# The up-projections of a gated feed-forward block by Strassen's seven products of quarters, with the weights' sums made by GpSimd

## The chip, the cores and the metric

One core of one Trainium2 chip runs the whole kernel. The metric is the device time of one execution in microseconds (us), as the median of several.

## The reference

Two transformer blocks run over 512 tokens of width 1024 in float32. The change concerns two gated feed-forward layers of the second block, here called GLU 1 and GLU 2:

```python
D_FF_2 = 2816
def swiglu(x, w1, w3, w2):
    return (jax.nn.silu(x @ w1) * (x @ w3)) @ w2
...
h = h + 0.5 * swiglu(rms_norm(h, ffn1_norm[l]), ffn1_w1[l], ffn1_w3[l], ffn1_w2[l])   # GLU 1
...
h = h + 0.5 * swiglu(rms_norm(h, ffn2_norm[l]), ffn2_w1[l], ffn2_w3[l], ffn2_w2[l])   # GLU 2
```

w1 and w3 are 1024 x 2816 ("gate" and "up", both up-projections), w2 is 2816 x 1024.

## The kernel before, in words

Everything is kept transposed: features on the 128 partitions, the 512 tokens along the free dimension, in two halves of 256 tokens (`hf` 0 and 1, `F` for both). Every float32 operand is split into a high part in the fp32r type and a low rest: for weights ScalarE writes the high part (`act_hi`, a Copy) and VectorE the low one (`dve_lo`, raw minus high). One product is then three matmuls into the same PSUM region, high by high, high by low and low by high (`mm3`), each with its own weight load of 128 x 128.

Weights come by DMA from SP's queue, in the order of `PLAN`, into three raw slots of 8 KB a partition (`NRAW`). A slot is loaded again when VectorE has made the low part of what lay in it. The split weights lie in three pairs of buffers (`NW`); the high part of weight w waits for the last matmul that used weight w-3 (`("used", w - NW)`). `act_step` and `dve_step` call for the splits two weights ahead. All five engines run their instructions strictly in the order written in `act_program`, `dve_program` and so on; a wait holds back all that stands behind it on that engine.

In a GLU, `pe_gate` works in 11 chunks of 256 features. A chunk takes one weight tile of w1 and one of w3 (each 1024 x 256, so 2 tiles of 128 features by 8 slices of the 1024 inputs by 3 matmuls, 48 matmuls of 512 tokens). Chunk 0 is made in two halves of 256 tokens (96 matmuls of 256 columns for each half), because the RMS norm of the second half is still being worked out beside it (`act_opening`, `dve_opening`, `dve_normed`, `act_normed`, `pool_normed`, with two scratch tiles `td` that go round for the normed input). ScalarE applies SiLU out of PSUM, VectorE multiplies by the other projection, then the product is split in high and low again (`act_hidden`, `dve_hidden`). w2 follows in three blocks of 8, 8 and 6 slices (`pe_linear`), each block one stage of chunks later than the chunks that it uses, and the last four outputs of the last block again in halves of 256 tokens, so that the next norm can start. In GLU 1 VectorE also scales the residual stream X by the last norm of the first block, eight instructions that stand in `dve_glu` after the first four chunks. PSUM has eight banks, handed out in turn by `banks`. GpSimd does little in the GLUs: some of the low parts of the normed input (`pool_normed`).

## Time and profile before

| what | us |
| --- | --- |
| median of 3 runs | 2319.98 (2315.99 to 2324.92) |
| the profiled execution, its own time | 2314.78 |
| its span, from the first to the last instruction | 2313.0 |
| TensorE (PE) busy in the span | 2228.9 |
| VectorE (DVE) busy | 1173.9 |
| ScalarE (ACT) busy | 825.9 |
| GpSimd (POOL) busy | 179.8 |

Busy time of PE is modelled, since matmuls are pipelined: what one matmul costs is read from the distance between two events that matmuls release, not from its duration. PEld is the weight load. SP issues the DMAs. The granted clock is TensorE's clock as a share of 2.4 GHz: 1.00 is 2.4 GHz and 0.50 is 1.2 GHz. A few per cent of the matmul records are missing from the trace, so counts in windows are a little low. A row of the timeline merges neighbouring instructions of one line, and names the shape of the first alone.

### The profile page before, as it was taken

Reading aid. Unit: us, or ns where it says so; the run is one execution under the profiler, and the core shown is the slowest. Engines: PE = TensorE matmul, PEld = TensorE weight load, DVE = VectorE, ACT = ScalarE, POOL = GpSimd, SP = SyncE. Lnnn points to the kernel's source line nnn. Section 1 sums busy time; section 2 is a strip of 40 time slices with the busy share of each in tenths; the row PEclk is TensorE's granted clock in tenths of the full one; section 3 lists DMA queues with packets and bytes.
Section 4 is the critical chain, followed back from the end, with each engine's and each line's share of the span. In section 5 each row is a group of like instructions: output and inputs, shape, how many; then the busy total and the mean of one; then the engine's idle time right before and its main releaser. Section 6 shows DMA issues by size and latency. Waiting matters only on the chain.

```text
span 2313.0 us, 27926 instructions
## 1 busy us (share of the span) xinstructions
PE 2228.9 (96%) x11611; PEld 1886.9 (82%) x11611; DVE 1173.9 (51%) x1845; ACT 825.9 (36%) x1241; POOL 179.8 (8%) x155
## 2 busy tenths in 40 slices
PE   6998999999999899999999999999999999999998
PEld 3877988888897788888898888887778889888887
DVE  5676566556577664334353433344664445333334
ACT  3555342213256543223243222234443324222222
POOL 7210000000033000000020000002012001000000
PEclk8999999999999999999999999999999999999999
DMA  6442255555520222322313232224112331422320
GB/s 230 141 140 85 93 171 180 190 180 185 189 74 19 86 80 91 109 91 91 110 55 110 91 109 91 82 73 120 57 32 73 119 110 56 127 92 92 109 73 37
DMA packets 144099, 245.45 MB, mean 106 GB/s; under 512 B 4763, under 2 KB 69622, under 8 KB 143846
## 3 DMA queue, kind: packets, MB, share of 16 engines
q1 hardware_dynamic: 139216, 228.02, 29.7%
q0 software_dynamic: 4096, 15.28, 2.0%
q8 instruction: 92, 1.51, 0.3%
q10 hardware_dynamic: 662, 0.37, 0.1%
q14 instruction: 33, 0.27, 0.0%
HBM read 241.56 MB, written 2.10 MB: 105 GB/s over the span
## 4 chain that ended last, share of the span: by engine, by line
PE 88%; DVE 6%; ACT 3%; issue 1%; DMA 1%; POOL 0%; SPq 0%; DVEq 0%; ACTq 0%
PE PS L66 87%; ACT t L72 3%; DVE t L83 2%; DVE t L86 1%; DVE t L75 1%; PE PS L69 1%; DMA t<-in_w_ada_dram 1%; DVE t L79 1%; POOL t L75 0%; DVE t L92 0%; DVE t L80 0%; SPq L101 0%; DVE t L95 0%; ACT L72 0%; DVEq L58 0%
## 5 line engine op out<-in xcount | busy, mean ns | idle before, releaser
L66 PE MATMUL PS<-t,t 128*128 128x512 f32 (+4 forms) x11244 | 2180.0, 357 | 53.3 <-ACT t L72 16.3
L66 PEld LDWEIGHTS PS<-t,t 128*128 128x128 f32 (+2 forms) x11244 | 1844.1, 188 | 386.2 <-issue 61.3
L72 ACT ACTIVATE t<-t 128x2048 fp32r<-128x2048 f32 (+10 forms) x551 | 527.7, 972 | 1174.0 <-PE PS L66 691.3
L75 DVE TENSOR_TENSOR t<-t,t 128x2048 fp32r<-128x2048 f32 (+8 forms) x476 | 581.9, 1227 | 650.9 <-ACT t L72 648.8
L72 ACT ACTIVATE t<-PS 128x512 f32<-128x512 f32 (+5 forms) x307 | 162.3, 545 | 183.0 <-PE PS L66 123.5
L75 POOL TENSOR_TENSOR t<-t,t 128x512 f32<-128x512 f32 (+2 forms) x71 | 88.1, 1242 | 1136.7 <-ACT t L72 962.7
L83 DVE SCALAR_TENSOR_TENSOR t<-t,t,t 128x1024 f32<-128x1024 f32 (+2 forms) x149 | 140.5, 947 | 16.4 <-DMA t<-in_w_ada_dram 10.9
L72 ACT ACTIVATE t<-t,t 128x256 fp32r<-128x256 f32 (+5 forms) x212 | 112.4, 537 | 88.9 <-DVE t L83 45.7
L75 DVE TENSOR_TENSOR t<-t,PS 128x512 f32<-128x512 f32 (+2 forms) x92 | 54.6, 600 | 147.2 <-PE PS L66 140.8
L83 DVE SCALAR_TENSOR_TENSOR t<-PS,t,t 128x512 f32<-128x512 f32 (+3 forms) x120 | 76.9, 643 | 94.6 <-PE PS L66 84.7
L69 PE MATMUL PS<-t,t 128*128 128x128 f32 (+1 forms) x367 | 57.8, 296 | 26.9 <-DMA t<-in_x_dram 6.1
L69 PEld LDWEIGHTS PS<-t,t 128*128 128x128 f32 (+1 forms) x367 | 44.8, 151 | 35.6 <-issue 10.6
L83 DVE SCALAR_TENSOR_TENSOR t<-t,t,PS 128x256 f32<-128x256 f32 (+1 forms) x133 | 62.0, 488 | 21.0 <-PE PS L66 13.9
L83 DVE SCALAR_TENSOR_TENSOR t<-PS,t 128x512 f32<-128x512 f32 (+1 forms) x68 | 40.3, 595 | 59.2 <-PE PS L66 58.7
L75 DVE TENSOR_TENSOR t<-t 128x512 f32<-128x512 f32 (+3 forms) x99 | 56.6, 572 | 23.0 <-ACT t L72 22.4
L79 DVE TENSOR_SCALAR t<-t,t 128x128 f32<-128x128 f32 (+5 forms) x159 | 56.5, 388 | 5.2 <-DMA t<-in_w_ada_dram 2.7
L79 POOL TENSOR_SCALAR t<-t 128x512 f32<-128x512 f32 x28 | 46.5, 1659 | 72.8 <-DVE t L86 48.5
L86 DVE CUSTOM_DVE_ANT_0 t<-PS,t 128x128 f32<-128x128 f32 (+1 forms) x112 | 38.5, 352 | 16.0 <-PE PS L66 15.8
L75 DVE TENSOR_TENSOR t<-PS,t 128x512 fp32r<-128x512 f32 (+2 forms) x40 | 25.0, 634 | 33.9 <-ACT t L72 23.5
L101 POOL DMA_DIRECT2D t<-in_k_dist_dram x1 | 0.5, 543 | 427.3 <-PE PS L66 427.3
L86 DVE CUSTOM_DVE_ANT_0 t<-PS,t,t 128x384 f32<-128x384 f32 (+3 forms) x56 | 29.3, 522 | 2.0
L72 ACT ACTIVATE t<-PS,t 128x2 f32<-128x2 f32 (+3 forms) x44 | 19.0, 431 | 29.0 <-PE PS L66 28.4
(30 smaller groups left out, 154.2 us busy)
## 6 DMA issues: line engine op xcount, KB each, us to landing
t<-in_w_ff_dram SPq DMA_DIRECT2D x64, 1024.0 KB, 5.3
t<-in_ffn_w_dram SPq DMA_DIRECT2D x60, 1024.0 KB, 5.2
t<-in_w_ada_dram SPq DMA_DIRECT2D x36, 1024.0 KB, 6.1
t<-in_w_in_dram SPq DMA_DIRECT2D x13, 1024.0 KB, 5.0
t<-in_w_ada_dram POOLq DMA_DIRECT2D x24, 512.0 KB, 4.4
t<-in_swa_w_qkv_dram SPq DMA_DIRECT2D x6, 1024.0 KB, 5.9
t<-in_ffn_w_dram SPq DMA_DIRECT2D x8, 768.0 KB, 4.2
t<-in_w_in_dram SPq DMA_DIRECT2D x24, 256.0 KB, 3.6
```

Source lines behind the costliest of these rows:

```text
L66: return Instr(self.real and self.real.matmul(o, lhs, rhs, start=start, stop=stop, **more))
L69: return Instr(self.real and self.real.transpose(o, src, ident))
L72: return Instr(self.real and self.real.activation(o, src, func, **more))
L75: return Instr(self.real and self.real.tensor_tensor(o, a, b, op))
L79: return Instr(self.real and self.real.tensor_scalar(o, a, s1, s2, op0))
L83: return Instr(self.real and self.real.scalar_tensor_tensor(o, a, s, b, op0, op1))
L86: return Instr(self.real and self.real.tensor_tensor_reduce(**more))
L101: return Instr(self.real and self.real.dma_start(o, src))
```

## The change

Chunk 0 (256 features) stays as it was. The remaining 2560 features are taken in five chunks of 512, for w1 and w3 each, which makes ten units for a GLU. For a unit the weights W (1024 x 512) and the normed input H (1024 x 512 tokens) are cut in 2 x 2 quarters, and the four output quarters come of seven products of quarters, each of 512 inputs by 256 features by 256 tokens: 2 x 4 x 3 = 24 matmuls of 256 columns. Four of the seven take sums of weight quarters, which GpSimd makes out of the raw weights (`pool_sum`, 128 x 1024 each); ScalarE and VectorE split each of the seven left operands (128 x 1024 instead of 128 x 2048). Four take sums of input quarters, made and split once for a GLU (`dve_t_sum`, `pool_t_sum`, `act_t_hi`, `dve_t_lo`), for which the normed input is kept in float32 (`H32`) and no longer in the two scratch tiles. Partial results are kept by ScalarE (`act_keep`) and joined by VectorE (`dve_join`). The split weights now lie in six half-size buffers; `AFTER` and `AHEAD` say which weight frees a buffer and how far ahead the splits may run. A unit has two raw loads: the first is released at the low part of product 4, the second at that of product 6. The blocks of w2 are now 6, 8 and 8 slices, and each comes directly after the units of its stage. The scaling of X in GLU 1 stands between chunk 0 and the first unit. `OUT` moves in memory. Cut to its core (whatever is not shown renames, or hands the same calls new arguments):

```diff
+        def unit(name, w, n0):
+            p0, w0 = len(PLAN), len(WT)
+            WX.setdefault(name, []).append(w0)
+            for m in range(7):
+                WT.append(dict(kt=4, nc=256, parts=None, wide=256, p=p0 + (m > 0), m=m, u=(p0, p0 + 1)))
+            for half, last in ((0, 4), (1, 6)):
+                LOADS[len(PLAN)] = (w[:, 4 * half:4 * half + 4, n0:n0 + 512], 4, 512, False)
+                PLAN.append(("w", w0 + last))
...
+        AT, AFTER, AHEAD, holders, turn = [], [], [], [None] * (2 * NW), 0
+        for w, it in enumerate(WT):
+            n = 2 if it["m"] is None else 1
+            turn += turn % n
+            a = turn % (2 * NW)
+            AT.append(a)
+            AFTER.append([v for v in sorted({-1 if v is None else v for v in holders[a:a + n]}) if v >= 0])
+            holders[a:a + n] = [w] * n
+            turn += n
+        for w in range(len(WT)):
+            v = w
+            while v + 1 < len(WT) and all(u < w for u in AFTER[v + 1]):
+                v += 1
+            AHEAD.append(v)
...
+        def pool_sum(e, w0, m):
+            w = w0 + m
+            a11, a12, a21, a22 = quarters(w)
+            dst, last = UL32[AT[w]][:, :, :], UL32[AT[w - 1]][:, :, :]
+            for before in AFTER[w]:
+                e.wait_ge(acc, ("used", before))
+            for p in WT[w]["u"]:
+                e.wait_ge(landed[SLOT[p]], p)
+            if m == 1:
+                e.tensor_tensor(dst, a21, a22, ALU.add).then_inc(summed, w)
+            elif m == 2:
+                e.wait_ge(summed, w - 1)
+                e.tensor_tensor(dst, last, a11, ALU.subtract).then_inc(summed, w)
+            elif m == 3:
+                e.wait_ge(summed, w - 1)
+                e.tensor_tensor(dst, a12, last, ALU.subtract).then_inc(summed, w)
+            else:
+                e.tensor_tensor(dst, a11, a21, ALU.subtract).then_inc(summed, w)
...
+        def dve_t_sum(e, i, n, N):
+            h = H32[i - 1]
+            e.wait_ge(hmul, (N, 7, 1))
+            if n == 1:
+                e.tensor_tensor(TL32[0][:, :, :], quarter_h(h, 0, 1), quarter_h(h, 0, 0), ALU.subtract).then_inc(
+                    t_sum, (i, 1))
+            elif n == 2:
+                e.wait_ge(t_sum, (i, 1))
+                e.tensor_tensor(TL32[1][:, :, :], quarter_h(h, 1, 1), TL32[0][:, :, :], ALU.subtract).then_inc(
+                    t_sum, (i, 2))
+            else:
+                if i == 1:
+                    e.wait_ge(x_up, ("first", 7))
+                e.tensor_tensor(TL32[2][:, :, :], quarter_h(h, 1, 1), quarter_h(h, 0, 1), ALU.subtract).then_inc(
+                    t_sum, (i, 3))
+        def pool_t_sum(e, i, N):
+            b21 = quarter_h(H32[i - 1], 1, 0)
+            e.wait_ge(t_sum, (i, 2))
+            e.wait_ge(h_lo, (N, 6, 0))
+            e.wait_ge(h_lo_pool, (N, 7, 0))
+            e.tensor_tensor(b21, b21, TL32[1][:, :, :], ALU.subtract).then_inc(t_pool, (i, 4))
...
+        def pe_unit(e, i, c, gate, nm):
+            u, w0 = (i, c, gate), g_unit(i, c, gate)
+            taken = sqr if gate else relu
+            banks.take((u, "x"), (taken, (u, Q21)), keep=True)
+            banks.take((u, "y"), (joined, (u, Q12)), keep=True)
+            banks.take((u, "z"), (joined, (u, Q11)), keep=True)
+            def product(m, name, bh, bl, first):
+                w = w0 + m
+                e.wait_ge(hi, w)
+                e.wait_ge(lo, w)
+                b = banks[u, name]
+                for n in range(2):
+                    for k in range(4):
+                        cs = slice(128 * n, 128 * n + 128)
+                        o = PS[:, b, 256 * n:256 * n + 256]
+                        ah, al = whi(w)[:, k, cs], wlo(w)[:, k, cs]
+                        e.matmul(o, ah, bh[:, k, :], start=first and n == k == 0, stop=False, skip_group_check=True)
+                        e.matmul(o, ah, bl[:, k, :], start=False, stop=False, skip_group_check=True)
+                        t = e.matmul(o, al, bh[:, k, :], start=False, stop=k == 3, skip_group_check=True)
+                t.then_inc(acc, (u, m), ("used", w))
+            def of_h(r, t):
+                for k in range(4 * r, 4 * r + 4):
+                    e.wait_ge(h_hi, (nm["N"], k, t))
+                    e.wait_ge(h_lo_pool if k % 2 else h_lo, (nm["N"], k, t))
+                return quarter_h(HHI, r, t), quarter_h(HLO, r, t)
+            def of_t(n):
+                e.wait_ge(t_lo, (i, n))
+                return TH[n - 1], TL[n - 1]
+            e.wait_for(banks.free((u, "x")))
+            product(0, "x", *of_h(0, 0), True)
+            e.wait_for(banks.free((u, "y")))
+            product(1, "y", *of_t(1), True)
+            e.wait_ge(copied, (u, 1))
+            product(2, "x", *of_t(2), False)
+            e.wait_ge(copied, (u, 3))
+            product(3, "y", *of_h(1, 1), False)
+            e.wait_ge(copied, (u, 2))
+            product(4, "x", *of_t(3), False)
+            e.wait_for(banks.free((u, "z")))
+            product(5, "z", *of_h(1, 0), True)
+            e.wait_ge(joined, (u, Q22))
+            e.wait_ge(t_lo, (i, 4))
+            product(6, "x", quarter_h(HHI, 0, 1), quarter_h(HLO, 0, 1), False)
+            for name in "xyz":
+                banks.open((u, name))
...
+        def act_keep(e, u, v, m, name, q):
+            ta.take((u, q), ((sqr if u[2] else relu), (u, q)))
+            e.wait_ge(acc, (u, m))
+            e.wait_for(ta.free((u, q)))
+            e.activation(quarter_tmp((u, q)), quarter_ps((u, name)), ACT.Copy).then_inc(copied, (u, v))
+        def act_take(e, u, q):
+            i, c, gate = u
+            s = g_slot(i, c)
+            if gate:
+                e.wait_ge(sqr, (u, q))
+                e.activation(quarter_of(GH[s], q), quarter_of(GL32[s], q), ACT.Copy).then_inc(hid_hi, (u, q))
+                return
+            if q == Q21:
+                e.wait_ge(acc, (u, 6))
+                src = quarter_ps((u, "x"))
+            else:
+                e.wait_ge(joined, (u, q))
+                src = quarter_tmp((u, q))
+            if c == 2:
+                e.wait_ge(t_lo, (i, 4))
+            e.activation(quarter_of(GL32[s], q), src, ACT.Silu).then_inc(relu, (u, q))
...
+        def act_unit(e, i, c, gate):
+            u, w0 = (i, c, gate), g_unit(i, c, gate)
+            act_split(e, AHEAD[w0] - 1)
+            act_keep(e, u, 1, 0, "x", Q11)
+            act_split(e, AHEAD[w0 + 1] - 1)
+            act_keep(e, u, 3, 1, "y", Q22)
+            if (c, gate) == (1, 0):
+                act_t_hi(e, i, 3)
+            act_split(e, AHEAD[w0 + 2] - 1)
+            act_keep(e, u, 2, 2, "x", Q12)
+            if (c, gate) == (1, 0):
+                act_t_hi(e, i, 4)
+            act_split(e, AHEAD[w0 + 3] - 1)
+            act_split(e, AHEAD[w0 + 4] - 1)
+            act_take(e, u, Q12)
+            act_split(e, AHEAD[w0 + 5] - 1)
+            act_take(e, u, Q22)
+            act_split(e, AHEAD[w0 + 6] - 1)
+            act_take(e, u, Q11)
+            act_take(e, u, Q21)
...
+        def dve_join(e, u, m, name, q, v):
+            tm = quarter_tmp((u, q))
+            e.wait_ge(acc, (u, m))
+            e.wait_ge(copied, (u, v))
+            e.tensor_tensor(tm, tm, quarter_ps((u, name)), ALU.add).then_inc(joined, (u, q))
+        def dve_times(e, u, q):
+            i, c, gate = u
+            if gate:
+                g = quarter_of(GL32[g_slot(i, c)], q)
+                e.wait_ge(relu, ((i, c, 0), q))
+                if q == Q21:
+                    e.wait_ge(acc, (u, 6))
+                    e.tensor_tensor(g, g, quarter_ps((u, "x")), ALU.mult).then_inc(sqr, (u, q))
                 else:
...
+                    e.wait_ge(joined, (u, q))
+                    e.tensor_tensor(g, g, quarter_tmp((u, q)), ALU.mult).then_inc(sqr, (u, q))
+        def dve_low(e, u, q):
+            i, c, gate = u
+            if gate:
+                s = g_slot(i, c)
+                e.wait_ge(hid_hi, (u, q))
+                e.tensor_tensor(quarter_of(GL[s], q), quarter_of(GL32[s], q), quarter_of(GH[s], q).bitcast(F32),
+                                ALU.subtract).then_inc(hid_lo, (u, q))
+        def dve_unit(e, i, c, gate, nm):
+            u, w0 = (i, c, gate), g_unit(i, c, gate)
+            dve_split(e, AHEAD[w0] - 1)
+            if (c, gate) == (1, 0):
+                dve_t_sum(e, i, 3, nm["N"])
+            dve_split(e, AHEAD[w0 + 1] - 1)
+            if (c, gate) == (1, 0):
+                dve_t_lo(e, i, 3)
+            dve_split(e, AHEAD[w0 + 2] - 1)
+            if (c, gate) == (1, 0):
+                dve_t_lo(e, i, 4)
+            dve_split(e, AHEAD[w0 + 3] - 1)
+            dve_join(e, u, 3, "y", Q12, 2)
+            dve_split(e, AHEAD[w0 + 4] - 1)
+            dve_times(e, u, Q12)
+            dve_join(e, u, 4, "x", Q22, 3)
+            dve_split(e, AHEAD[w0 + 5] - 1)
+            dve_times(e, u, Q22)
+            dve_low(e, u, Q12)
+            dve_join(e, u, 5, "z", Q11, 1)
+            dve_split(e, AHEAD[w0 + 6] - 1)
+            dve_times(e, u, Q11)
+            dve_low(e, u, Q22)
+            dve_low(e, u, Q11)
+            dve_times(e, u, Q21)
+            dve_low(e, u, Q21)
...
+            ws = g_ws(i)
+            act_opening(e, nm, ws)
+            act_split(e, g_unit(i, 1, 0))
+            act_gate(e, i, 0)
+            act_t_hi(e, i, 1)
+            act_t_hi(e, i, 2)
+            act_gate(e, i, 1)
...
         def dve_glu(e, i, nm, nxt, before):
-            dve_gate(e, i, 0, nm)
+            ws = g_ws(i)
+            dve_opening(e, nm, ws)
+            dve_split(e, g_unit(i, 1, 0))
+            dve_t_sum(e, i, 1, nm["N"])
+            dve_t_sum(e, i, 2, nm["N"])
+            dve_gate(e, i, 0)
+            dve_t_lo(e, i, 1)
+            dve_t_lo(e, i, 2)
+            dve_gate(e, i, 1)
+            dve_split(e, AHEAD[ws[1]])
...
+        def pool_glu(e, i, nm):
+            pool_glu_norm(e, nm)
+            for n, w0 in enumerate(WX[f"s{i}"]):
+                pool_sum(e, w0, 1)
+                if n == 0:
+                    pool_t_sum(e, i, nm["N"])
+                pool_sum(e, w0, 2)
+                pool_sum(e, w0, 3)
+                pool_sum(e, w0, 4)
```

## Rows read from the trace of the kernel before

**Rows 1.** The page, part 1: busy us, share of the span, instructions.
```profile
PE 2228.9 (96%) x11611; PEld 1886.9 (82%) x11611; DVE 1173.9 (51%) x1845; ACT 825.9 (36%) x1241; POOL 179.8 (8%) x155
```

**Rows 2.** Windows over most of GLU 1 and GLU 2: busy us, records, clock, DMA.
```profile
1205.00:1562.00 357.00, 355.42 (x1676) 298.69 (x1676) 137.27 (x145) 96.29 (x105) 2.95 (x4) 1.00 0.29 93
1942.00:2300.00 358.00, 357.17 (x1714) 301.69 (x1714) 131.18 (x140) 95.10 (x103) 2.95 (x4) 1.00 0.27 86
```

**Rows 3.** Waits of PE, longest in total: us, times, longest.
```profile
PE PS L66 <- ACT t L72: 16.3, 14, 3.0
...
PE PS L66 <- DVE t L75: 8.1, 6, 3.1
```

**Rows 4.** Timeline of ACT in GLU 1: start us, us, engine, instruction, idle before.
```profile
1247.46 1.92 ACT L72 ACTIVATE t<-t 128x2048 fp32r<-128x2048 f32 x1 [7.71 <-PE PS L66]
...
1269.22 1.92 ACT L72 ACTIVATE t<-t 128x2048 fp32r<-128x2048 f32 x1 [7.71 <-PE PS L66]
...
1519.46 1.49 ACT L72 ACTIVATE t<-t 128x1536 fp32r<-128x1536 f32 x1 [9.39 <-PE PS L66]
1527.62 1.49 ACT L72 ACTIVATE t<-t 128x1536 fp32r<-128x1536 f32 x1 [6.67 <-PE PS L66]
```

**Rows 5.** Timeline of DVE, released by groups of 256-column matmuls (GLU 1's end, GLU 2's chunk 0).
```profile
1543.27 0.42 DVE L83 SCALAR_TENSOR_TENSOR t<-PS,t 128x256 f32<-128x256 f32 x1 [0.32 <-PE PS L66]
...
1544.35 0.42 DVE L83 SCALAR_TENSOR_TENSOR t<-PS,t 128x256 f32<-128x256 f32 x1 [0.32 <-PE PS L66]
...
1956.85 0.42 DVE L75 TENSOR_TENSOR t<-t,PS 128x256 f32<-128x256 f32 x1 [1.69 <-PE PS L66]
...
1959.73 0.42 DVE L75 TENSOR_TENSOR t<-t,PS 128x256 f32<-128x256 f32 x1 [1.55 <-PE PS L66]
```

**Rows 6.** Groups by shape, ACT and DVE, whole span: count, busy us, mean ns.
```profile
L72 ACT ACTIVATE t<-t 128x1024 fp32r<-128x1024 f32 x2 | 2.1, 1046 | 0.0
...
L72 ACT ACTIVATE t<-PS 128x512 f32<-128x512 f32 x200 | 116.5, 589 | 123.7 <-PE PS L66 71.4 <-PE PS L69 36.1 <-DVE t L75 11.7
L72 ACT ACTIVATE t<-t 128x512 fp32r<-128x512 f32 x120 | 75.4, 632 | 256.3 <-DVE t L75 237.2 <-DVE t L83 10.0 <-DVE t L79 8.9
...
L75 DVE TENSOR_TENSOR t<-t,t 128x1024 fp32r<-128x1024 f32 x2 | 2.4, 1221 | 0.3 <-ACT t L72 0.3
...
L75 DVE TENSOR_TENSOR t<-t,PS 128x512 f32<-128x512 f32 x72 | 48.9, 686 | 97.5 <-PE PS L66 91.2 <-POOL t L75 5.9
```

**Rows 7.** Timeline of POOL: additions and subtractions of two tiles.
```profile
1593.81 1.29 POOL L75 TENSOR_TENSOR t<-t,t 128x512 f32<-128x512 f32 x1 [17.77 <-PE PS L66]
...
1606.39 2.36 POOL L75 TENSOR_TENSOR t<-t,t 128x512 f32<-128x512 f32 x1 [7.77 <-PE PS L66]
...
1948.63 0.74 POOL L75 TENSOR_TENSOR t<-t,t 128x256 fp32r<-128x256 f32 x1 [1.04 <-ACT t L72]
```

**Rows 8.** The page, part 6: DMA issues, KB each, us to landing.
```profile
t<-in_ffn_w_dram SPq DMA_DIRECT2D x60, 1024.0 KB, 5.2
```

**Rows 9.** Timeline of DVE in GLU 1: the scaling of X.
```profile
1282.11 5.38 DVE L83 SCALAR_TENSOR_TENSOR t<-t,t,t 128x512 f32<-128x512 f32 x8
```

**Rows 10.** Windows around idle stretches of PE: columns as in rows 2.
```profile
1192.00:1194.00 2.00, 2.00 (x12) 2.00 (x11) 1.36 (x4) 1.06 (x1) 0.00 (x0) 0.50 0.00 0
...
1612.00:1614.00 2.00, 0.00 (x0) 0.00 (x0) 0.53 (x2) 1.98 (x3) 0.00 (x0) 0.96 0.00 0
1614.00:1616.00 2.00, 1.84 (x3) 0.84 (x3) 1.41 (x1) 0.59 (x2) 0.00 (x0) 0.50 0.00 0
1616.00:1618.00 2.00, 2.00 (x8) 1.57 (x7) 1.08 (x2) 0.00 (x0) 1.28 (x1) 0.68 0.68 193
```

**Rows 11.** Timeline of GLU 1's chunk 0, all engines.
```profile
1185.76 1.32 PE L66 MATMUL PS<-t,t 128*128 128x256 f32 x6 [0.87 <-DVE t L75]
...
1204.06 1.28 ACT L72 ACT_TABLE_LOAD   x1
...
1205.79 19.58 PE L66 MATMUL PS<-t,t 128*128 128x256 f32 x119 [1.30 <-ACT t L72]
```

More of the change, by code:

```diff
@@ L635, in act_step @@
             if split:
-                act_split(e, w + 2)
+                act_split(e, AHEAD[w])
         def dve_step(e, w, split=True):
@@ new lines, in act_gate @@
+        def act_gate(e, i, hf):
+            s = g_slot(i, 0)
+            for n in range(2):
+                k1, k3 = (("g", i), 0, n, hf), (("g", i), 1, n, hf)
+                ta.take(k3, (hid_lo, k3))
+                tm = TMP[ta[k3]][:, COLS[hf]]
+                e.wait_ge(acc, k1)
+                e.wait_for(ta.free(k3))
+                e.activation(tm, PS[:, banks[k1], COLS[hf]], ACT.Silu).then_inc(relu, k1)
+                e.wait_ge(sqr, k3)
+                e.activation(GH[s][:, n, COLS[hf]], tm, ACT.Copy).then_inc(hid_hi, k3)
@@ L2276, in dve_glu @@
             for blk in range(3):
-                if blk < 2:
-                    dve_gate(e, i, blk + 1, nm)
+                for c in GUNITS[blk]:
+                    dve_unit(e, i, c, 0, nm)
+                    dve_unit(e, i, c, 1, nm)
                 for n2 in range(2):
```

303 lines of the change are left out of this document (181 added, 122 removed).

## The prediction

> **What bounds the kernel now.** I read the page's busy line first: TensorE is busy for 96% of the span, VectorE for half, ScalarE for a third, GpSimd for 8% [rows 1]. The windows over the two GLUs are denser still: PE is busy for 355.4 of 357 us and 357.2 of 358 us at full clock, with VectorE at about 38%, ScalarE at 27% and the DMA engines at under 30% [rows 2]. In the waits of PE its longest cause adds up to 16 us over the whole kernel [rows 3]. So a GLU lasts as long as its matmuls take to stream, and the change is worth what it takes off that stream less the waits it brings.
>
> What a matmul costs is read from events that it releases. ScalarE's 128x2048 copy waits for PE in every chunk, at 1247.46 and again at 1269.22 [rows 4]: 21.76 us for a chunk of 96 matmuls of 512 columns, 226.7 ns each (the w2 weight of 36 matmuls that ends between 1519.46 and 1527.62 gives 8.16 us, the same). Matmuls of 256 columns occur in chunk 0 and in the last w2 outputs: two VectorE instructions released 9 of them apart start at 1543.27 and 1544.35, and two released 24 apart at 1956.85 and 1959.73 [rows 5]. That is 1.08/9 and 2.88/24 us, 120.0 ns each. Half the columns cost 53%, not 50%: both prices are the columns at 2.4 GHz plus 13.3 ns.
>
> **The sum, part by part.**
>
> *Products.* Two chunks of 256 features (one 512-feature chunk for w1 or w3) are now 96 matmuls of 512 columns, 21.76 us. A unit is 7 x 24 = 168 matmuls of 256 columns, 168 x 0.120 = 20.16 us. The scheme takes off an eighth of the arithmetic, but the fixed part of each matmul is paid 168 times and not 96, so 7.4% is left: 1.60 us a unit, 20 units, -32.0 us.
>
> A rule on this price: the Trainium skill (TensorE: Matmul & The Clock Gate, "Back-to-back issue gap") gives an isolated matmul its columns at 2.4 GHz plus 2.5 ns. By that a unit would fall from 20.7 to 18.4 us and the sum to about -47; the cadences above contradict it here.
>
> *w2.* The w2 slices are as many as before (22), but the last block has 8 and not 6, and its last four outputs go in halves: 24 matmuls of 512 (5.44 us) become 48 of 256 (5.76 us). +0.3 a GLU, +0.6.
>
> *Opening.* The normed input goes to `H32`, so VectorE no longer waits for a scratch tile. Before, PE idles at 1185.76 and again for 1.30 us at 1205.79, where a PSUM bank waits for ScalarE's first SiLU, which stands behind a 128x2048 split and a table load [rows 11]. That split becomes one of 128x1024 (1.05 us instead of 1.92 [rows 4, 6]) and the norm in front of it ends some 0.9 us sooner. I take 1.3 us off there and 0.4 us at each opening: -2.1 (bounds 0 and -4, all such idle time).
>
> *Supply of the units, VectorE and ScalarE.* For a gate unit, w3's, VectorE has seven low parts at 1.22 us, three joins and four products at 0.69, four lows at 0.69 [rows 6]: 16.1 of 20.16 us. ScalarE has seven highs at 1.05, three keeps at 0.59 and four copies at 0.63: 11.7 us. Neither is full, but they work in order and for each other. Walking the queues with these durations: VectorE's last low of a w3 unit ends about 5 us into the next unit and ScalarE about 4 us, so the next unit's split of product 4 and then its first keep end at about 5.75 us; product 2, due at 5.76, waits for that keep. It is just in time, as is product 6 (due at 17.3, its join ends at 17.3). This handover from a w3 to a w1 unit occurs twice a GLU; elsewhere w2's stage lies between, four weights of 8.2 or 10.9 us, in which the queues catch up. I take 0.25 us each, +1.0. If handshakes or the strided quarters cost a fifth more than my rows, each of the 20 units waits 0.5 to 1 us: +10 to +20.
>
> *Supply, GpSimd.* An addition of two tiles takes 0.74 us for 256 columns and 1.29 for 512 [rows 7], so by extension 2.4 us for 1024. The row for a 512-column one that is stretched to 2.36 us gives the upper bound, 4.7 us. Four sums a unit are 9.6 us (bound 19). The loop that matters: a unit's second raw load starts when the previous unit's low part of product 4 is done; it lands 5.2 us later [rows 8] (0.3 to issue), then four sums, one high (1.05), one low (1.22). 5.5 + 9.6 + 2.3 = 17.4 us, under 20.16. It is hidden at 2.4 us a sum and begins to show at 3.1.
>
> *Entering the first unit.* Its first six splits stand behind chunk 0's last low parts: product 1 waits some 0.3 us, in both GLUs. In GLU 1 the eight scalings of X, 5.38 us in a row [rows 9], have moved from under four chunks' cover to a place ahead of `dve_unit`, so they stand before the low part of product 4 and before the third input sum. From chunk 0's end as zero: lows 1 to 3 done at 5.3, scalings at 10.7, low 4 at 11.8, sum at 13.0, its high on ScalarE at 14.1; behind that, in ScalarE's order, product 6's high and the keep that product 4 waits for, at 15.7. Product 4 is due at 12.0: a wait of 3.7 us. In GLU 2 the same chain without the scalings ends before product 4 is due. Such a gap is dear: after 2 us of idle at 1612 the granted clock is 0.50 for the next 2 us and 0.68 in the 2 after [rows 10], and it was 0.50 at 1192 behind the short gaps of GLU 1's opening [rows 10, 11]; half speed over some 3.4 us (2 + 0.64 x 2 by these rows) costs 1.7 us. So GLU 1 pays 0.3 + 3.7 + 1.7 = 5.7 (bounds 0.3 if VectorE gets there in time, 9 if product 6 waits too), GLU 2 0.4.
>
> *DMA, the rest.* The bytes are the same, in as many loads less a few. Outside the GLUs the half-size buffers hand out the same lookahead, three whole tiles. Both nothing.
>
> Sum: -32.0 + 0.6 - 2.1 + 1.0 + 5.7 + 0.4 = -26.4 us. The profiled span of 2313.0 becomes 2286.6, an execution of 2288.4 with the 1.8 us that lie around it. That execution was 5.2 us under the median of the runs, 2319.98, so the median becomes 2293.6, say 2294.
>
> **Rivals.**
>
> *A. VectorE and ScalarE are late in every unit.* The margins above are zero at two places, and I summed durations with few handshakes. Against it: VectorE has 4 us of air in a w3 unit and 9 in a w1 unit. Price +10 to +20: 2304 to 2314, around the border of "no change".
>
> *B. GpSimd's sums set the pace; slower than before.* Place: the raw-load loop. With g = 7.8 + 4t - 20.16 us of excess for a sum of t us, a run of four units gathers 3g, less about 2 us of air; for both GLUs (two runs of four and one of two each) 2 x (7g - 6) = 14g - 12. It eats the gain of 26 from g = 2.7, t = 3.8 us. At the stretched 4.7 us g is 6.4: +78 us, 2372. For it: the stretched row, and that GpSimd now works beside a VectorE that is 60 to 80% busy. Against it: the rows of 0.74 and 1.29 us lie beside a working VectorE too. On the skill's side (GPSIMD Engine Reference, section 3.1) a 2048-column addition is measured at 4497 ns, an estimate of 2.3 us for half of it, and the page's rule is to leave elementwise work to VectorE as about twice as fast; this trace's 1.29 against 0.69 us agrees.
>
> *C. All is hidden, the scalings too.* Only the first three terms are left: -32.0 + 0.6 - 2.1, and up to 2 more at the openings. 2284 to 2287.
>
> *D. The shorter matmul is cheaper in a long stream,* by the page's rule named above: a saving nearer -47, about 2279. All cadences speak against it.
>
> **How the numbers follow.** My forecast (2286 to 2303) gets 0.60, A 0.18, B 0.08, C 0.11, D 0.03. The time is that of the forecast, 2294. Range 2282 to 2310: it leaves out B, D and the upper third of A. A change of 0.5% is 11.6 us, about what a measurement of this kernel can tell from none: under 2308.4 is faster, which holds the forecast, C, D and nearly half of A, 0.82. Within it: the rest of A, 0.10. Above 2331.6: B, 0.08.
>
> **What the profile after would show.** Splits 20.16 us apart from unit to unit, products released 2.88 us apart. About 3360 more matmuls of 256 columns and 1920 fewer of 512. GpSimd sums of about 2.4 us, 80 of them, near 195 us more busy time. One idle stretch of PE of some 4 us in the first unit of GLU 1, ended by ScalarE, with the clock at half behind it, and none in GLU 2. The prediction is wrong if units are further apart than 20.5 us, if PE waits for ScalarE's splits of products 1 to 4 (then GpSimd or the raw load is late), or if 256-column matmuls with three products adding into one bank cost other than 120 ns.

## The result and the profile after

The kernel became slower by 1.3%: 2349.56 us (2347.37 to 2351.27, four runs) against 2318.32 us (2315.99 to 2324.92) before, a ratio of 1.013 with a 95% interval of 1.0106 to 1.0153. The prediction was 2294 us, and faster. The profiled execution took 2349.82 us, with a span of 2347.8.

From the page, the busy line and the chain that ended last:

```profile
PE 2218.3 (94%) x13099; PEld 1951.6 (83%) x13099; DVE 1380.4 (59%) x2019; ACT 933.1 (40%) x1409; POOL 403.1 (17%) x237
...
PE 75%; DVE 10%; ACT 5%; POOL 4%; issue 4%; DMA 3%; SPq 0%; POOLq 0%; DVEq 0%; ACTq 0%
```

TensorE fell from 96% [rows 1] to 94%. In the chain VectorE went from 6% to 10% and GpSimd from 0 to 4%. The windows from within GLU 1's chunk 0 to near the end of that GLU, and over a like stretch of GLU 2 (length, then busy time with count for PE, PEld, DVE, ACT, POOL, granted clock, DMA share, GB/s):

```profile
1206.98:1560.00 353.02, 327.85 (x2272) 308.73 (x2273) 223.33 (x202) 141.56 (x170) 107.41 (x40) 0.98 0.29 95
1972.00:2319.00 347.00, 325.73 (x2243) 307.02 (x2242) 215.43 (x190) 138.25 (x167) 108.72 (x40) 0.96 0.26 86
```

PE was busy for all but 1 or 2 us of such windows before [rows 2]; now it idles for 25 us in one and 21 in the other. From the opening of chunk 0 to the end of its w2, GLU 1 went from 376.8 to 394.9 us and GLU 2 from 366.6 to 384.0: +18.0 and +17.5, all of the loss. The waits of PE by cause (total us, times, longest):

```profile
PE PS L66 <- DVE t L75: 50.0, 22, 8.1
PE PS L66 <- ACT t L72: 20.3, 17, 3.0
```

Before, the two came to 8.1 and 16.3 us. So PE waits for VectorE. The timeline of PE over the first units of GLU 1 shows that it does so again and again (in brackets the idle time before the row):

```profile
1222.20 10.89 PE L66 MATMUL PS<-t,t 128*128 128x256 f32 x72 [6.33 <-DVE t L75]
1234.47 6.02 PE L66 MATMUL PS<-t,t 128*128 128x256 f32 x48 [1.38 <-ACT t L72]
1244.16 21.77 PE L66 MATMUL PS<-t,t 128*128 128x256 f32 x168 [3.68 <-DVE t L75]
1268.77 8.89 PE L66 MATMUL PS<-t,t 128*128 128x256 f32 x72 [2.84 <-DVE t L75]
1279.67 11.78 PE L66 MATMUL PS<-t,t 128*128 128x256 f32 x96 [2.00 <-ACT t L72]
```

The row of 168 matmuls has as many as a unit, without a gap: product 6 of the first unit and products 0 to 5 of the second. It takes 21.77 us from the first start to the modelled end, because the granted clock behind the gap was 0.50 for 2 us and 0.68 for 2 more. In the full-speed stretches the releases lie 2.88 us apart for 24 matmuls, as before [rows 5]. The matmul price held.

The gaps lie at few places. Those ahead of 1244.16, 1268.77 and 1293.75 stand before product 6 of the first three units and end with VectorE's join (the last of these joins ends at 1293.70). The gap ahead of 1279.67 stands before product 2 of the third unit, the first behind a w3 unit, and ends with ScalarE's keep at 1279.62. These are the two places that the prediction called "just in time".

What VectorE does when it is late is seen in a timeline of 9 us, from the end of the first unit into the second:

```profile
1242.29 1.22 DVE L75 TENSOR_TENSOR t<-t,t 128x1024 fp32r<-128x1024 f32 x1 [1.73 <-POOL t L75]
1243.43 0.68 DVE L75 TENSOR_TENSOR t<-t,PS 128x512 f32<-128x512 f32 x1
...
1245.69 2.39 POOL L75 TENSOR_TENSOR t<-t 128x1024 f32<-128x1024 f32 x1
1245.83 1.06 ACT L72 ACTIVATE t<-t 128x1024 fp32r<-128x1024 f32 x1 [1.05 <-POOL t L75]
1245.84 3.33 DVE L75 TENSOR_TENSOR t<-t,t 128x1024 fp32r<-128x1024 f32 x1 [1.73 <-POOL t L75]
1249.09 0.68 DVE L75 TENSOR_TENSOR t<-t,PS 128x512 f32<-128x512 f32 x1
1249.69 1.21 DVE L75 TENSOR_TENSOR t<-t,t 128x1024 fp32r<-128x1024 f32 x1
```

The low part of 128x1024 that starts at 1245.84 lasts 3.33 us. The next one, at 1249.69, lasts 1.21, and before the change it was 1.22 [rows 6]. GpSimd's sum began 0.15 us ahead of the long one, at 1245.69, and ended at 1248.08; the long one ended at 1249.17, 1.09 us later, about its own length. It looks as if VectorE stood still until GpSimd had finished. VectorE is also late in a second way: the low part at 1242.29 had waited 1.73 us for a sum to be made, and the join that ended PE's gap of 3.68 us stands right behind it, at 1243.43. ScalarE's 1.06 us at 1245.83 is not touched. The groups by shape show what kind of instruction is hit (busy us, mean ns, then idle before):

```profile
L75 DVE TENSOR_TENSOR t<-t,t 128x1024 fp32r<-128x1024 f32 x150 | 246.9, 1656 | 176.0 <-POOL t L75 91.6 <-ACT t L72 84.4
...
L75 POOL TENSOR_TENSOR t<-t,t 128x1024 f32<-128x1024 f32 x62 | 170.0, 2743 | 366.8 <-PE PS L66 227.8 <-DMA t<-in_ffn_w_dram 127.3 <-DVE t L75 7.1
...
L75 DVE TENSOR_TENSOR t<-t,PS 128x512 f32<-128x512 f32 x102 | 69.0, 681 | 14.2 <-PE PS L66 8.0 <-POOL t L75 4.4
...
L75 DVE TENSOR_TENSOR t<-t,t 128x512 f32<-128x512 f32 x59 | 49.1, 833 | 1.9 <-DVE t L75 0.5
```

VectorE's 128x1024 low parts went from 1221 ns to a mean of 1656. Its 128x512 instructions with both inputs in SBUF and a float32 output went from 686 to 833 ns, and those with one input in PSUM stayed at 681 (686 before). The 128x512 low parts, with fp32r output and both inputs in SBUF too, stayed at 700 ns (701 before); at the first handover, where the trace shows them (1273.71 to 1278.91), GpSimd stood idle. GpSimd's sums, 2.39 us undisturbed, have a mean of 2743 ns in the group shown and of 2630 in the other 20. Each engine holds up the other, whichever comes second. The Trainium skill (SBUF — State Buffer, "SBUF: two separate sides") states just this: VectorE and GpSimd share a pair of ports, held for a whole instruction by whichever starts first, and a VectorE instruction with two SBUF inputs needs it against a GpSimd instruction that reads SBUF. The trace agrees, with 3.33 against 1.21 us for the one kind and 681 against 686 ns for the other.

Entering the first unit is hit hardest. These are VectorE's rows from short stretches of its timeline, and GpSimd's of the same time:

```profile
1209.43 1.74 DVE L75 TENSOR_TENSOR t<-t,t 128x256 fp32r<-128x256 f32 x1 [0.48 <-ACT t L72]
...
1211.09 3.42 DVE L75 TENSOR_TENSOR t<-t,t 128x1024 fp32r<-128x1024 f32 x1
...
1214.43 3.40 DVE L75 TENSOR_TENSOR t<-t,t 128x1024 fp32r<-128x1024 f32 x1
...
1219.88 0.43 DVE L75 TENSOR_TENSOR t<-t,t 128x256 fp32r<-128x256 f32 x1 [0.48 <-ACT t L72]
```

```profile
1205.96 7.47 POOL L75 TENSOR_TENSOR t<-t,t 128x1024 f32<-128x1024 f32 x3 [3.56 <-DVE t L75]
1213.39 3.36 POOL L75 TENSOR_TENSOR t<-t 128x1024 f32<-128x1024 f32 x1
```

Beside four additions of GpSimd (one of the input, three of the weights) a low part of 256 columns takes 1.74 us, where the free one at 1219.88 takes 0.43, and the two low parts of the input sums (`dve_t_lo`) take 3.42 and 3.40. The second gates of chunk 0 stand behind them in VectorE's order, and the low parts of products 1 to 3 behind those. So PE idles for 6.33 us before product 1, at 1222.20 (8.09 us in GLU 2).

The trace of before already held the sign. One row of it stood in the prediction's own evidence: GpSimd's addition of 2.36 us at 1606.39 [rows 7]. Beside it VectorE made a low part:

```profile
1605.31 2.29 DVE L75 TENSOR_TENSOR t<-t,t 128x2048 fp32r<-128x2048 f32 x1 [1.91 <-ACT t L72]
```

The low part ended at 1607.60, and the addition 1.15 us after that, about its own undisturbed length of 1.29 us. Here GpSimd came second. The other way round is in rows that the prediction did not use: GpSimd's 256-column addition in GLU 1's opening, VectorE's two-input instruction beside it, and one of the same shape with GpSimd idle:

```profile
1182.30 0.74 POOL L75 TENSOR_TENSOR t<-t,t 128x256 f32<-128x256 f32 x1 [0.97 <-ACT t L72]
1182.45 0.87 DVE L75 TENSOR_TENSOR t<-t,t 128x256 f32<-128x256 f32 x1
...
1183.89 0.42 DVE L75 TENSOR_TENSOR t<-t,t 128x256 f32<-128x256 f32 x1
```

0.87 us and 0.42 us: the first ended 0.28 us after GpSimd's 0.74 us were over. Instructions this short lost 0.2 to 0.5 us each, in a few places (VectorE's at 1166.78, 1169.66, 1181.01 and 1182.45).

### The profile page after: what moved, and what is told of

It is laid out like the page before. It is cut to its first block, busy times and chain, and to the rows that moved or that the text cites. A ratio compares the mean times of both kernels' runs of the same rounds, so it can differ in the third digit from the quotient of the medians.

```text
span 2347.8 us, 31535 instructions
## 1 busy us (share of the span) xinstructions
PE 2218.3 (94%) x13099; PEld 1951.6 (83%) x13099; DVE 1380.4 (59%) x2019; ACT 933.1 (40%) x1409; POOL 403.1 (17%) x237
## 4 chain that ended last, share of the span: by engine, by line
PE 75%; DVE 10%; ACT 5%; POOL 4%; issue 4%; DMA 3%; SPq 0%; POOLq 0%; DVEq 0%; ACTq 0%
PE PS L66 74%; DVE t L75 5%; ACT t L72 5%; POOL t L75 4%; DVE t L83 2%; DMA t<-in_ffn_w_dram 2%; DVE t L86 1%; PE PS L69 1%; DMA t<-in_w_ada_dram 1%; DVE t L79 1%; DVE t L80 0%; DVE t L92 0%; SPq L101 0%; DVE t L95 0%; POOLq L58 0%
## 5 line engine op out<-in xcount | busy, mean ns | idle before, releaser
L66 PE MATMUL PS<-t,t 128*128 128x256 f32 (+4 forms) x12732 | 2167.9, 333 | 100.0 <-DVE t L75 50.0
L66 PEld LDWEIGHTS PS<-t,t 128*128 128x128 f32 (+2 forms) x12732 | 1907.2, 191 | 357.8 <-issue 74.1
L75 DVE TENSOR_TENSOR t<-t,t 128x1024 fp32r<-128x1024 f32 (+7 forms) x616 | 770.7, 1263 | 578.3 <-ACT t L72 481.0
L72 ACT ACTIVATE t<-t 128x2048 fp32r<-128x2048 f32 (+8 forms) x689 | 623.0, 920 | 1057.2 <-PE PS L66 437.6
L75 POOL TENSOR_TENSOR t<-t,t 128x1024 f32<-128x1024 f32 (+3 forms) x133 | 258.1, 1942 | 1214.1 <-ACT t L72 675.1
L72 ACT ACTIVATE t<-PS 128x512 f32<-128x512 f32 (+4 forms) x337 | 180.7, 552 | 227.5 <-PE PS L66 166.3
L83 DVE SCALAR_TENSOR_TENSOR t<-t,t,t 128x1024 f32<-128x1024 f32 (+2 forms) x149 | 140.4, 947 | 16.1 <-DMA t<-in_w_ada_dram 10.6
L75 DVE TENSOR_TENSOR t<-t,PS 128x512 f32<-128x512 f32 (+2 forms) x122 | 74.6, 616 | 56.0 <-PE PS L66 49.8
L75 DVE TENSOR_TENSOR t<-t 128x512 f32<-128x512 f32 (+4 forms) x103 | 61.4, 596 | 23.7 <-ACT t L72 23.0
L75 POOL TENSOR_TENSOR t<-t 128x1024 f32<-128x1024 f32 x20 | 52.6, 2630 | 18.6 <-PE PS L66 18.6
L86 DVE CUSTOM_DVE_ANT_0 t<-PS,t 128x128 f32<-128x128 f32 (+1 forms) x112 | 38.4, 352 | 18.3 <-PE PS L66 18.1
```

The costliest lines, as they stand in the source:

```text
L66: return Instr(self.real and self.real.matmul(o, lhs, rhs, start=start, stop=stop, **more))
L72: return Instr(self.real and self.real.activation(o, src, func, **more))
L75: return Instr(self.real and self.real.tensor_tensor(o, a, b, op))
L83: return Instr(self.real and self.real.scalar_tensor_tensor(o, a, s, b, op0, op1))
L86: return Instr(self.real and self.real.tensor_tensor_reduce(**more))
```

## Experiments

Every kernel was run four to ten times beside the kernel before, whose medians lay between 2317.1 and 2318.5 us. "Ratio" is to that kernel, with its 95% interval. The groups of runs were made on different chips, so a difference of a microsecond or two between kernels says little.

| kernel | sums made by | median us (range) | ratio [95%] |
| --- | --- | --- | --- |
| the change | GpSimd | 2349.56 (2347.37 to 2351.27) | 1.0130 [1.0106, 1.0153] |
| e1_nosums | nobody | 2292.36 (2291.28 to 2296.23) | 0.9891 [0.9875, 0.9907] |
| e7_nosums_noscale | nobody, 7 scalings out | 2287.26 (2283.77 to 2289.16) | 0.9867 [0.9852, 0.9881] |
| e2_memset | memsets, 2.86 us | 2327.26 (2320.00 to 2328.18) | 1.0034 [1.0015, 1.0054] |
| e9_memset24 | memsets, 2.43 us | 2309.09 (2307.42 to 2309.48) | 0.9962 [0.9948, 0.9976] |
| e10_memset24_early | memsets, early load | 2295.91 (2295.60 to 2296.37) | 0.9906 [0.9891, 0.9921] |
| e4_early | GpSimd, early load | 2334.81 (2331.41 to 2337.40) | 1.0070 [1.0054, 1.0087] |
| e5_dvesums | VectorE | 2324.44 (2323.22 to 2329.37) | 1.0032 [1.0018, 1.0046] |
| e6_best | VectorE, early, scalings moved | 2324.58 (2322.24 to 2325.85) | 1.0025 [1.0015, 1.0034] |
| e12_v7 | as e6, entry reordered | 2319.43 (2311.53 to 2320.53) | 0.9998 [0.9987, 1.0009] |
| e11_v6 | as e12, first keep ahead | 2291.63 (2289.26 to 2295.89) | 0.9889 [0.9874, 0.9904] |
| e13_v6_late | as e11, late load | 2293.16 (2291.76 to 2295.11) | 0.9889 [0.9874, 0.9904] |
| e14_pool_order | GpSimd, early, keep ahead | 2357.77 (2356.45 to 2359.41) | 1.0165 [1.0144, 1.0187] |

**Without the sums (e1_nosums).** Every product takes a plain quarter, GpSimd makes none of the 80 sums; matmuls, splits, keeps and joins stay.

```diff
-            src = UL32[AT[w]][:, :, :] if m in (1, 2, 3, 4) else {0: a11, 5: a12, 6: a22}[m]
+            src = [a11, a22, a12, a22, a11, a12, a22][m]
```

> Leaves out GpSimd's 80 sums of weight quarters: products 1 to 4 take plain quarters, so the output is not the reference's; all matmuls, splits, keeps and joins stay. Theory L (lock): an instruction of VectorE with two SBUF inputs and a GpSimd sum exclude each other, and this lengthens VectorE's queue until PE waits. Theory R (raw-load loop): the sums only add their own length to the loop from a unit's second raw load to the next, without slowing VectorE. Both expect most of the excess gone: 2290 to 2305 us, units 20.2 us apart. Theory S (the start of each GLU, its scalings and half clock are what costs): 2335 to 2345, since those stay.

2292.36 us: within 2 us of the forecast of 2294. VectorE's low parts are back at 1223 ns. In the first 70 us of the units PE idles twice, before product 1 and at the scalings:

```profile
1217.62 8.86 PE L66 MATMUL PS<-t,t 128*128 128x256 f32 x72 [0.74 <-DVE t L75]
1229.89 60.31 PE L66 MATMUL PS<-t,t 128*128 128x256 f32 x489 [3.41 <-ACT t L72]
```

So all of the loss, and the whole gap to the forecast (57 us from run to run), comes with the sums.

**Memsets for sums (e2_memset, e9_memset24).** The same places, waits and signals, but GpSimd writes a constant and reads nothing. First three whole memsets (954 ns each), then two whole and one of half size, together 2.43 us, near the 2.39 to 2.41 us of a real sum. With the steps between them the three span 2.55 us. The code of the second form, cut:

```diff
-                e.tensor_tensor(dst, a21, a22, ALU.add).then_inc(summed, w)
...
+            e.memset(dst, 0.001).then_inc(spare, (w, 0))
+            e.wait_ge(spare, (w, 0))
+            e.memset(dst[:, :, 0:128], 0.001).then_inc(spare, (w, 1))
+            e.wait_ge(spare, (w, 1))
+            e.memset(dst, 0.001).then_inc(summed, w)
```

> In place of each sum GpSimd makes three memsets of the same 128x1024 buffer, one after the other, which read nothing from SBUF (the sums' values are left out, the output is not the reference's). All waits and the loop are as in the changed kernel. Theory L: VectorE's 128x1024 low parts go back from a mean of 1.66 us to 1.22 us although GpSimd is as busy, and the time is near that without sums, 2290 to 2310. Theory R: if the three memsets last 2.4 us or more, the loop is as long as before and the time stays at 2335 to 2350 with VectorE undisturbed.

> As the run with three memsets for each sum, but the second covers an eighth to a half of the buffer only (128x512 of 1024 columns), so that the three together last near the 2.4 us of an undisturbed sum (estimate 0.95 + 0.5 + 0.95). GpSimd is busy as in the changed kernel and reads nothing, so nothing is blocked. The difference to the changed kernel's 2349.6 us is the price of the blocking at equal length. Theory L puts nearly all on it: 2295 to 2305. Theory R puts most on the queues that wait for the sums one after the other: 2310 to 2325, as the run with 2.86 us for a sum gave 2327.

The times were 2327.26 us (five runs, two at 2320 and three at 2327 to 2328) and 2309.09 us. Both lie between the ranges of the two theories, so both effects are at work. In the groups of e9_memset24 VectorE's low parts are undisturbed while GpSimd is just as busy:

```profile
L75 DVE TENSOR_TENSOR t<-t,t 128x1024 fp32r<-128x1024 f32 x150 | 182.4, 1224 | 205.7 <-ACT t L72 108.8 <-POOL t L98 96.9
...
L98 POOL MEMSET t<- 128x1024 f32 x160 | 150.5, 953 | 357.5 <-PE PS L66 257.1 <-DMA t<-in_ffn_w_dram 95.8
```

With about the length of a sum kept and its reading gone, 2349.56 becomes 2309.09: blocking costs 40.5 us (39 by the ratios). PE's wait before product 1 of the first unit falls with it, from 6.33 us to 0.48. The length counts too: 0.43 us more a sum, 18.2 us more in all. By that price the 0.15 us that the memsets span more than a sum hide some 6 us of blocking (an estimate), so 40.5 is rather too low. And 16.7 us stay over e1_nosums, which no blocking explains. Most of them are the raw-load loop (13.2, below). It is seen in the timeline of GpSimd in e9_memset24 (four sums of one unit, then the next units'), and in that of VectorE and SP's queue:

```profile
1251.06 2.55 POOL L98 MEMSET t<- 128x1024 f32 x3 [8.83 <-PE PS L66]
1253.94 2.54 POOL L98 MEMSET t<- 128x1024 f32 x3 [0.33 <-PE PS L66]
1256.82 2.55 POOL L98 MEMSET t<- 128x1024 f32 x3 [0.34 <-PE PS L66]
1259.70 2.55 POOL L98 MEMSET t<- 128x1024 f32 x3 [0.33 <-PE PS L66]
1276.85 10.01 POOL L98 MEMSET t<- 128x1024 f32 x12 [14.60 <-DMA t<-in_ffn_w_dram]
```

```profile
1269.00 1.23 DVE L75 TENSOR_TENSOR t<-t,t 128x1024 fp32r<-128x1024 f32 x1 [0.25 <-ACT t L72]
...
1270.26 0.37 SPq L101 DMA_DIRECT2D t<-in_ffn_w_dram  x1
```

The last sum ends at 1262.25. The low part of product 4, on which the raw slot waits, starts only at 1269.00: it stands in VectorE's order behind the outgoing unit's joins, products and low parts, and so does the high part that it needs on ScalarE (it ends just before). The load is issued at 1270.26 and the next sums start at 1276.85. That is 11.2 us for four sums (they wait for their buffers, 2.88 us apart, as PE frees them), 8.0 for the low part and 6.6 for the load: 25.8 us for a loop that had 20.16, at this handover from a w3 to a w1 unit.

**The raw half released at the sums (e4_early, e10_memset24_early).** The first half of the next raw load waits for the sum of product 4 and the low part of product 0, the last readers of that half, not for the low part of product 4.

```diff
-                        e.wait_ge(lo, old[1])
+                        m = WT[old[1]]["m"]
+                        if m == 4:
+                            e.wait_ge(lo, old[1] - 4)
+                            e.wait_ge(summed, old[1])
+                        else:
+                            e.wait_ge(lo, old[1])
```

> The changed kernel with one wait moved: SP loads over a unit's first raw half when the sum of product 4 is made (and product 0 split), no longer when VectorE has made product 4's low part. Complete computation. Theory R: the loop gets 2.3 us and more shorter for each of 14 transitions, 30 us at most: 2320 or less. Theory L: loads come earlier but VectorE is blocked as before: 2335 to 2348.

> The same memsets of 2.4 us, and the first raw half released early as in the run with the moved wait. Theory R: with the loop shortened and nothing blocked no more than the sums' own length is left, and it is hidden: 2292 to 2300. Its difference to the run with the moved wait alone (2334.8) is again the blocking.

With real sums 2334.81, 14.8 us less than the change; with memsets 2295.91, 13.2 less than e9_memset24. GpSimd's waits for the raw load (127.3 us in the change, 95.8 in e9_memset24) are gone in both. Between the two, sums against memsets of the same length, lie 38.9 us: the blocking again, by a second pair.

**Without seven of the eight scalings of X (e7_nosums_noscale).** As e1_nosums, and X is scaled in one slice alone.

> Without sums, as in the first experiment, and seven of the eight scalings of X in GLU 1 left out. It prices the prediction's term for the scalings: the idle stretch of 3.4 us in the first unit of GLU 1 and the half clock behind it should go, 3 to 6 us under the 2292.4 of the run with the scalings.

2287.26, 5.1 us under e1_nosums; the idle stretch of 3.41 us is gone. The forecast had 5.4 us for it (3.7 and the clock's 1.7). The first unit of GLU 2 has no such stretch in e1_nosums, as predicted.

**The sums on VectorE (e5_dvesums).** All that GpSimd summed is done by VectorE, with low parts one split behind so that a sum's high and low don't wait for each other.

```diff
...
+            while dve_at["s"] <= upto:
+                w = dve_at["s"]
+                if WT[w]["m"] in (1, 2, 3, 4):
+                    pool_sum(e, w - WT[w]["m"], WT[w]["m"])
+                dve_at["s"] += 1
...
```

> The changed kernel with all sums made by VectorE (1.22 us each, one split ahead of the low parts), GpSimd idle in the units. Complete computation. VectorE then has 21.0 us of work in a w3 unit of 20.16 and 17 in a w1 unit. Theory L: VectorE loses 4.9 us a unit to the sums but is freed of 9.6 us of blocking: 2295 to 2315. If nothing blocked it (theory R), the added load would count in full and the loop get shorter: low parts stay at 1.66 us in the mean.

2324.44: 25 us better than the change, though VectorE now makes all 80 sums as well, but short of the expected 2295 to 2315. A sum takes it 1.23 us; on GpSimd it took 2.4 and held VectorE up. The low parts are at 1222 ns. PE's first rows in GLU 1:

```profile
1221.97 7.61 PE L66 MATMUL PS<-t,t 128*128 128x256 f32 x48 [6.37 <-DVE t L75]
1232.22 42.07 PE L66 MATMUL PS<-t,t 128*128 128x256 f32 x336 [2.65 <-ACT t L72]
1277.62 12.62 PE L66 MATMUL PS<-t,t 128*128 128x256 f32 x81 [3.33 <-ACT t L72]
```

The 3.33 us come four times, at each handover from a w3 to a w1 unit, and are ended by ScalarE: one of the places that the prediction had called "just in time". VectorE's queue has grown, and a margin of zero does not carry it. The entry is no better than in the change (6.37 us), and VectorE's own sums now stand in its queue there.

**Order of the queues (e6_best, e12_v7, e11_v6, e13_v6_late).** All with sums on VectorE. e6_best adds the early release and moves the scalings ahead of chunk 0's second gates. e12_v7 also splits products 1 to 3 before chunk 0's last gates. e11_v6 lets ScalarE's first keep of each unit go ahead of the split of product 4, and at the w3 to w1 handovers defers two quarters' copies and low parts to behind it:

```diff
-            act_split(e, AHEAD[w0] - 1)
             act_keep(e, u, 1, 0, "x", Q11)
+            if c in (2, 4) and not gate:
+                act_take(e, (i, c - 1, 1), Q11)
+                act_take(e, (i, c - 1, 1), Q21)
+            act_split(e, AHEAD[w0] - 1)
...
```

e13_v6_late is e11_v6 with the raw half released at the low part of product 4, as in the change.

> Complete computation, meant to beat both kernels: all sums on VectorE, the first raw half released early, the scalings of X ahead of chunk 0's second half, the splits of products 1 to 3 ahead of chunk 0's last gates, and at the handover from a w3 unit to a w1 unit ScalarE's first keep ahead of the takes of two quarters that VectorE is late with. The sums on VectorE alone gave 2324 with idle stretches of PE of 6.4 us at each GLU's first unit, 2.7 us at the scalings and 3.3 us at four handovers, with half clock behind them. If those are what is left, 30 us and more go: 2290 to 2300. If VectorE is simply full (18.6 of 20.16 us a unit in the mean), waits come back elsewhere: 2310 to 2325.

> The fastest version (2291.6) without its change at the handover from a w3 to a w1 unit: ScalarE's first keep stands again behind the split of product 4 and behind the takes that wait for VectorE. Four handovers in the kernel; each cost 3.3 us of idle PE in the run with the sums on VectorE alone, and up to 1.7 us of half clock behind it. Expected 2305 to 2312 if those come back, 2292 to 2296 if the early release has already made room.

> The sums on VectorE with the early release and the scalings moved, without the changed order at the first unit and at the handovers. Against the run above it prices the order at the first unit of a GLU: 6.4 us of idle PE and half clock in each of two GLUs, 2318 to 2322.

> The fastest version with the first raw half released late again, at the low part of product 4. With the sums on VectorE the four sums last 4.9 us and not 9.7 or more, so the raw-load loop has air: under 2295. If the loop still counts, 2300 to 2305.

e11_v6 took 2291.63 us and is the best complete version: 1.1% faster than the kernel before, 58 us under the change. Its groups (low parts and sums of VectorE) and PE's rows:

```profile
L75 DVE TENSOR_TENSOR t<-t,t 128x1024 fp32r<-128x1024 f32 x150 | 181.5, 1229 | 28.1 <-ACT t L72 24.9
...
L75 DVE TENSOR_TENSOR t<-t,t 128x1024 f32<-128x1024 f32 x64 | 78.1, 1220 | 26.6 <-PE PS L66 26.2
```

```profile
1210.45 8.89 PE L66 MATMUL PS<-t,t 128*128 128x256 f32 x72 [0.48 <-ACT t L72]
1223.08 67.12 PE L66 MATMUL PS<-t,t 128*128 128x256 f32 x537 [3.73 <-DVE t L75]
```

The handovers have no gap; the 3.73 us in the first unit of GLU 1, with the scalings ahead of the low parts, stay. In e12_v7 the gap is there, with the keep (1271.46, ACT from PSUM) behind the split of product 4 (1270.50) that had waited 1.95 us for VectorE:

```profile
1270.50 1.06 ACT L72 ACTIVATE t<-t 128x1024 fp32r<-128x1024 f32 x1 [1.95 <-DVE t L75]
1271.46 0.58 ACT L72 ACTIVATE t<-PS 128x512 f32<-128x512 f32 x1
...
1272.09 2.21 PEld L66 LDWEIGHTS PS<-t,t 128*128 128x128 f32 x10 [3.54 <-ACT t L72]
```

2319.43 against 2291.63: 27.8 us (25 by the ratios) for the place of one copy of 0.58 us in ScalarE's queue, with two quarters' copies and low parts deferred behind it. The 2305 to 2312 expected for e12_v7 priced a gap at 3.3 us and 1.7 of half clock. In the traces the four gaps of 3.34 us are 13.4 us, and the clock behind them costs 9.1 more: it is at 0.50 for 6 us behind each of the two gaps in GLU 1, and for less in GLU 2. The rest lies at the entries, where e12_v7 idles for 3.19 us in GLU 2's first unit. Whether the keep's place would do without the deferred quarters wasn't tried. The entry's order is worth 5.2 us (e6_best to e12_v7). e6_best itself came out no faster than e5_dvesums (2324.58; 2318 to 2322 were expected): with the scalings moved ahead, PE's one gap at GLU 1's entry is 9.36 us, where e5_dvesums has 6.37 and 2.65. The late release costs nothing once the sums run on VectorE (2293.16 and 2291.63, the same ratio): a sum of 1.22 us that stands right ahead of the low parts leaves the loop its air.

**GpSimd's sums with most of that order (e14_pool_order).** Early release, scalings moved, keep ahead and the two quarters deferred, the sums back on GpSimd. The splits of products 1 to 3 stay behind chunk 0's last gates, as in the change.

> GpSimd's sums kept, complete computation, with the early release of the first raw half, the scalings of X moved ahead of chunk 0's second half, and ScalarE's first keep ahead of the split of product 4. It asks whether order alone can hide the blocking. Theory L with the blocking at 39 us in the old order: the keeps no longer stand behind a blocked VectorE, but joins and low parts still do; 2310 to 2325, and never as low as the version with the sums on VectorE (2291.6). If the order is all, 2290 to 2300.

2357.77: slower than the change, and far above the 2310 to 2325 expected. PE's timeline in GLU 1 and the group of the low parts:

```profile
1231.05 17.27 PE L66 MATMUL PS<-t,t 128*128 128x256 f32 x120 [12.01 <-DVE t L75]
1251.15 21.73 PE L66 MATMUL PS<-t,t 128*128 128x256 f32 x168 [2.83 <-DVE t L75]
...
1300.84 95.37 PE L66 MATMUL PS<-t,t 128*128 128x256 f32 x648 [5.57 <-DVE t L75]
```

```profile
L75 DVE TENSOR_TENSOR t<-t,t 128x1024 fp32r<-128x1024 f32 x150 | 264.1, 1783 | 169.0 <-ACT t L72 113.7 <-POOL t L75 55.3
```

The low parts are blocked still more (1783 ns), and with the scalings ahead of it PE's gap at GLU 1's entry is 12.01 us. The two traces show where the 23 us over e4_early lie. In the first unit of GLU 1 PE idles for 14.8 us in e14_pool_order (12.01 and 2.83) and for 11.6 in e4_early (6.31, 3.27 and 2.03). Around the four handovers it idles for 30 us in e14_pool_order, four times 1.97 and 5.6, and for 13 us in e4_early. So most of it is the new order at the handovers, where the deferred low parts stand ahead of the next unit's joins, and little is the scalings. This order, which fits a free VectorE, does not hide the blocking.

## Why the prediction was wrong

The account from the change to the forecast, each term from one pair of runs:

| step | from, to | us |
| --- | --- | --- |
| GpSimd's reads and VectorE's two-input instructions block each other | change, e9_memset24 | 40.5 |
| the raw-load loop | e9_memset24, e10_memset24_early | 13.2 |
| what else the sums cost | e10_memset24_early, e1_nosums | 3.5 |
| all other terms of the sum | e1_nosums 2292.4, forecast 2294 | -1.6 |

**The step that failed: "Supply, GpSimd".** It concluded "It is hidden at 2.4 us a sum". The length of a sum was right (2.39 to 2.41 us undisturbed). Two things were not: the price of running it beside VectorE was put at nothing, without a reason, and the loop was summed too short.

First, the supply of VectorE was summed with its durations from the kernel before, as if nothing beside it changed. Low parts cost 1.66 us in the mean and up to 3.42, not 1.22. A w3 unit had 16.1 of 20.16 us on VectorE; seven low parts at 0.44 us more are 3.1 us, on top of two places whose margin was zero, product 2 behind a handover and product 6. PE's gaps stand at these. No rival held this: A allowed "a fifth more than my rows", by handshakes, and B looked only at how long GpSimd's sums get. The argument against B was that rows of 0.74 and 1.29 us "lie beside a working VectorE too". It did not ask what VectorE was doing: beside the row at 1593.81 it ran an instruction with one input in PSUM (1593.73, 0.70 us), and during the one at 1948.63 none with two inputs in SBUF. The row that did meet one is the stretched one, 2.36 us, which the prediction took for a bound on the length and not for a sign of blocking. Where GpSimd came first, it was VectorE's row that was stretched (0.87 for 0.42 us).

Second, the loop. The term "high (1.05), low (1.22)" between last sum and load took 8.0 us in e9_memset24, since the low part of product 4 has to pass all that stands before it in VectorE's order, and four sums took 11.2, not 9.6, since their buffers come free at PE's pace. 25.8 us, not 17.4, at such a handover. Rival B had the place right, and "begins to show at 3.1" us a sum was too high: it shows at 2.43.

Two slips in the working change nothing: 2 + 0.64 x 2 is 3.3 us and not 3.4, and by the rule set beside the matmul price a unit is 18.3 us and not 18.4. The last term of the table, -1.6 us, is a sum of several that were not all priced alone, so its smallness may be luck in part.

**Right, by the runs.** Products: 2.88 us for 24 matmuls, and e1_nosums lands at the sum, which it could not with -47 or 0 for that term; rival D falls, and a ratio of 0.9891 bears out a gain of 25 us. Scalings of X: 5.1 for 5.4 us. Opening: the wait of 1.30 us that was to go is gone in e1_nosums, but with the sums it is still there (1.28 us at 1206.98). DMA and the rest: nothing outside the GLUs, whose 18.0 and 17.5 us are all of the loss. VectorE and ScalarE at the handovers: "just in time" held with VectorE as it was (e1_nosums has no gap there, where the forecast had 1.0 us in all) and broke at the first extra load (3.33 us in e5_dvesums).

What remains open: whether the keep's place alone, without the deferred quarters, would close the handovers in e11_v6 and keep them short in e14_pool_order, and whether a GpSimd instruction with one SBUF input would block as these with two do. Neither was tried.

## What to carry to other kernels

Elementwise work with two inputs that is moved to an idle GpSimd is not free for a VectorE whose own instructions read two inputs from SBUF: here blocking beside 80 additions of 2.4 us cost 40 us. Made by VectorE itself, at 1.22 us each, they fit, but only once the queues had been put in another order (2291.6 us; 2324.4 in the old order). Before counting on a second engine, look in the trace for the same instruction of the first with and without it, and compare the single rows, not the means. And cost a loop through in-order queues from the place that each instruction has in its queue: a low part of 1.2 us ended 8 us after the sum that it needed, and one copy of 0.58 us moved ahead, with two quarters deferred behind it, was worth 25 to 28 us.
